# Gated delta rule on one core: squares of chunk outputs split in two parts and summed by two fp32r products

## The reference

```python
def step(state, xs):
    u_c, w_c, qd_c, kd_c, a_c, gl_c = xs
    v_new = u_c - w_c @ state
    o_c = qd_c @ state + a_c @ v_new
    state = state * gl_c + kd_c^T @ v_new
    return state, o_c
...
o = rmsnorm_2(o, out_norm) * silu(z)      # mean of squares over the 128 features of a head
return o.reshape(B, L, GDN_V_W) @ w_out
```

## Time and profile before

| | |
|---|---|
| median of 3 runs | 1943.84 us (1940.74 to 1944.12) |
| profiled execution | 1942.34 us, span 1939.6 us |
| TensorE busy | 1833.5 us, 95% |
| VectorE busy | 994.7 us, 51% |
| ScalarE busy | 822.8 us, 42% |
| GpSimd busy | 676.4 us, 35% |
| TensorE clock granted, mean | 0.985 |
| the four recurrences | 885 to 924, 1034 to 1086, 1197 to 1249, 1360 to 1412 us |

### The profile page before, as it was taken

One profiled execution on the slowest core, in us unless ns is written; L12 is line 12 of the kernel. 1 busy time (PEld: TensorE's weight loads), 2 busy tenths in 40 slices (PEclk: granted clock), 3 DMA queues, 4 the chain that ended last, 5 costly groups with the idle time before them and its releaser, 6 DMA issues.

```text
span 1939.6 us, 30688 instructions
## 1 busy us (share of the span) xinstructions
PE 1833.5 (95%) x11693; PEld 1538.4 (79%) x11829; DVE 994.7 (51%) x1753; ACT 822.8 (42%) x1503; POOL 676.4 (35%) x429
## 2 busy tenths in 40 slices
PE   6999999999999998998999999999978999999996
PEld 4777788888787876887989998998976667777776
DVE  6522233731111225665765774775766556566666
ACT  4566643352323233633633642562445443333433
POOL 3222244453534342270280263255224212222312
PEclk9999999999999998999999999999999999999998
DMA  5112133232323230420230131122132101221201
GB/s 186 55 55 66 55 98 109 66 98 68 118 80 105 86 99 21 137 79 1 80 89 23 55 91 48 52 80 78 34 111 76 55 33 55 65 55 53 76 32 44
DMA packets 73668, 138.90 MB, mean 72 GB/s; under 512 B 30640, under 2 KB 42416, under 8 KB 73296
## 3 DMA queue, kind: packets, MB, share of 16 engines
q1 hardware_dynamic: 72976, 132.41, 22.7%
q10 hardware_dynamic: 576, 4.87, 0.6%
HBM read 127.62 MB, written 9.63 MB: 71 GB/s over the span
## 4 chain that ended last, share of the span: by engine, by line
PE 44%; DVE 6%; POOL 5%; issue 3%; ACT 3%; DMA 0%; SPq 0%; ACTq 0%; POOLq 0%; DVEq 0%
PE ps L348 9%; PE ps L350 8%; PE ps L349 8%; PE ps L3092 4%; PE ps L3048 2%; POOL wsp L343 2%; PE ps L3055 2%; PE ps L3082 1%; POOL ov L836 1%; PE ps L2770 1%; POOL work L832 1%; PE ps L2874 1%; PE ps L2907 1%; PE ps L2912 1%; DVE aux_f L1789 1%
## 5 line engine op out<-in xcount | busy, mean ns | idle before, releaser
L343 POOL TENSOR_TENSOR wsp<-raw,wsp 128x1024 fp32r<-128x1024 f32 x228 | 549.8, 2418 | 1154.7 <-ACT wsp L338 1154.5
L348 PE MATMUL ps<-h_split,wsp 128*128 128x264 f32 (+2 forms) x1552 | 535.0, 345 | 16.8 <-DVE h_split L497 5.0
L349 PE MATMUL ps<-h_split,wsp 128*128 128x264 f32 (+2 forms) x1552 | 516.0, 332 | 0.0
L350 PE MATMUL ps<-h_split,wsp 128*128 128x264 f32 (+2 forms) x1552 | 515.6, 332 | 0.0
L348 PEld LDWEIGHTS ps<-h_split,wsp 128*128 128x128 f32 x1552 | 294.3, 190 | 58.2 <-issue 17.2
L349 PEld LDWEIGHTS ps<-h_split,wsp 128*128 128x128 f32 x1552 | 295.3, 190 | 28.8 <-issue 0.2
L350 PEld LDWEIGHTS ps<-h_split,wsp 128*128 128x128 f32 x1552 | 294.2, 190 | 29.2
L338 ACT ACTIVATE wsp<-raw 128x1024 fp32r<-128x1024 f32 x228 | 237.6, 1050 | 95.2 <-PE ps L350 94.5
L348 PE MATMUL ps<-y_split,wsp 128*128 128x512 f32 (+2 forms) x512 | 196.4, 384 | 11.5 <-DVE y_split L531 5.3
L349 PE MATMUL ps<-y_split,wsp 128*128 128x512 f32 (+2 forms) x512 | 192.5, 376 | 0.0
L350 PE MATMUL ps<-y_split,wsp 128*128 128x512 f32 (+2 forms) x512 | 192.0, 375 | 0.0
(11 more groups left out here) (391 smaller groups left out, 2929.6 us busy)
## 6 DMA issues: line engine op xcount, KB each, us to landing
raw<-in_w SPq DMA_DIRECT2D x228, 512.0 KB, 3.5
m_home<-ov SPq DMA_DIRECT2D x16, 256.0 KB, 3.5
x_home<-x_res ACTq DMA_DIRECT2D x1, 2112.0 KB, 6.9
x_res<-in_x SPq DMA_DIRECT2D x4, 512.0 KB, 5.3
out<-x_res SPq DMA_DIRECT2D x16, 128.0 KB, 1.7
x_res<-x_home ACTq DMA_DIRECT2D x1, 1584.0 KB, 7.4
mats<-in_mats SPq DMA_DIRECT2D x1, 640.0 KB, 7.4
x_res<-x_home ACTq DMA_DIRECT2D x1, 528.0 KB, 3.9
```

The lines of the kernel that those rows point to most:

```text
L343: pool.tensor_tensor(wsp[:, s, 1, :], raw[:, s, :], wsp[:, s, 0, :].bitcast(F32), ALU.subtract).then_inc(lo_ready, 1)
L348: pe.matmul(o, wh, xh, start=start, stop=False)
L349: pe.matmul(o, wh, xl, start=False, stop=False)
L350: return pe.matmul(o, wl, xh, start=False, stop=stop)
```

## The change

After the square, ScalarE copies it to an fp32r buffer `sq_hi`, VectorE subtracts that from the square into `sq_lo` (in place of the square), and TensorE sums both with a matrix of -1 in fp32r, in two products of all four heads at once instead of four fp32 products. The factor -1/128 goes into the logarithm's scale. `sq_hi` lies where RO lies, so the copy waits for the store of the chunk before. VectorE does its part for chunk c-1 behind VB of chunk c (and behind `copy_z(3)` for c = 1), ahead of R, and for the last chunk ahead of the four gate products. The semaphore of the last quarter of x is shared with that of x's copy to DRAM, whose waits count up to 32.

```diff
+        sq_hi, sq_lo = quad(yt, 6 * 512), quad(yt, 5 * 512)
...
+        def x_part(q):
+            return sem("x_moved") if q == 3 else sem(f"x_in{q}")
...
-                sp.dma_start(X[:, 2 * q:2 * q + 2, META:T], A["x"][:, 2 * q:2 * q + 2, :]).then_inc(sem(f"x_in{q}"), 16)
+                sp.dma_start(X[:, 2 * q:2 * q + 2, META:T], A["x"][:, 2 * q:2 * q + 2, :]).then_inc(x_part(q), 16)
...
-            norm_squares(act, "n1", lambda k: X[:, k, REAL], N1, ready=lambda k: (sem(f"x_in{k // 2}"), 16))
+            norm_squares(act, "n1", lambda k: X[:, k, REAL], N1, ready=lambda k: (x_part(k // 2), 16))
...
-                    act.activation(RO[:, :, 0:n], bank(2, n), ACT.Ln, bias=col("eps")).then_inc(sem("g_oln"), 1)
+                    act.activation(RO[:, :, 0:n], bank(2, n), ACT.Ln, bias=col("eps"), scale=-1.0 / P).then_inc(sem("g_oln"), 1)
...
                     act.activation(SQO[:, :, 0:n], bank(4, n), ACT.Square).then_inc(sem("g_sqo"), 1)
+                    act.wait_ge(sem("g_sqo"), 2 * at - 1)
+                    if c:
+                        act.wait_ge(sem("g_store"), at - 1)
+                    act.activation(sq_hi[:, :, 0:n], SQO[:, :, 0:n], ACT.Copy).then_inc(sem("g_sqo"), 1)
...
-                    act.wait_ge(sem("x_moved"), 16)
+                    act.wait_ge(sem("x_moved"), 32)
...
+                def square_low(c):
+                    n = tokens(c)[1]
+                    at = gst(g, CHUNKS, c + 1)
+                    dve.wait_ge(sem("g_sqo"), 2 * at)
+                    dve.tensor_tensor(sq_lo[:, :, 0:n], SQO[:, :, 0:n], sq_hi[:, :, 0:n].bitcast(F32), ALU.subtract)\
+                       .then_inc(sem("g_sq_lo"), 1)
...
                     if c:
+                        square_low(c - 1)
                         dve.wait_ge(sem("g_ks"), later)
...
+                square_low(LATER)
                 for t in range(4):
                     gate_y(t, LATER - 1)
                 add_out(6)
...
-                    pe.wait_ge(sem("g_sqo"), at)
+                    pe.wait_ge(sem("g_sqo"), 2 * at)
...
-                    for h in range(HG):
-                        last = pe.matmul(quads(2, h, P, n), mat(MEAN_128), SQO[:, h, 0:n], start=True, stop=True)
-                    last.then_inc(sem("g_on"), 1)
+                    total = PS[:, 2, :].rearrange("p (h n) -> p h n", h=HG)[:, :, 0:n]
+                    pe.matmul(total, ones_r[:, 1, :], sq_hi[:, :, 0:n], start=True, stop=False)
+                    pe.wait_ge(sem("g_sq_lo"), at)
+                    pe.matmul(total, ones_r[:, 1, :], sq_lo[:, :, 0:n], start=False, stop=True)\
+                      .then_inc(sem("g_on"), 1)
```

## The result

| | before | after |
|---|---|---|
| median | 1943.98 us (20 runs) | 1949.98 us (1940.98 to 1955.99, 20 runs) |
| ratio, 95% interval | | 1.0035 [1.0024, 1.0046] |
| profiled execution, span | 1942.34, 1939.6 us | 1949.95, 1947.9 us |
| granted clock, mean of that execution | 0.985 | 0.980 |

The change costs 6.0 us by the medians. The forecast was no change, 1943.7, within 1939.8 to 1948.0. The page of the changed kernel shows no sign of more work: TensorE's busy time is the same as before to 0.7 us, in 120 records less.

A forecast was written before the change was run, and what follows sets the result against it. TensorE was taken as the bound. Group 0's +0.9 us and -1.0 for groups 1 to 3 gave -0.1 against 1942.34, so 1942.2; with the median 1.5 above that execution, 1943.7, range 1939.8 to 1948.0.

The forecast's parts named there:

- 0.86: Norm pair on TensorE: upper bound in us if its two products stand alone between waits; 0.46 was forecast.
- 1.8 was summed: Groups 1 to 3, up to the last chunk: shorter norm products in line on TensorE save 1.8 us per group.
- rival (b): Norm pair not streamed, costs up to 0.86 us, so groups 1 to 3 save nothing on norms: 1949.2 us; chance 0.12.
- The gap of VectorE: Group 0, chunks 1 to 3: VectorE idles 0.73 us between VB and L2018; the new difference fits there, costing nothing.
- the 1.46 us that were drawn: Ends of groups 1 to 3: gates queue behind square, copy and difference, so add and TensorE come 1.46 us later.
- 0.16 and 0.75: Group 0: chunk 4 longer by 0.16 us, and TensorE freed 0.75 us later at the group's end.
- (a): Full gain: the gates' wait at the ends of groups 1 to 3 costs nothing; -4.5 us, 1939.3; chance 0.12.
- (c): Difference or gates meet GpSimd's L343 at three ends, up to 2.1 us each: 1945 to 1950 us; chance 0.06.
- rival (d): TensorE idles 2.4 us at three ends and its clock falls, 3.1 us each: 1953 us; chance 0.04.
- -1.8 + 1.46 = -0.34 per group: Groups 1 to 3: saving on the norms plus later end, net -0.34 us per group, -1.0 for three.
- -0.1: Whole kernel: group 0's +0.9 us and -1.0 for groups 1 to 3 sum to -0.1 us.

The follow-up runs named there:

- group 0 old: Changed kernel with group 0's four fp32 products and no split as in the kernel before, gates ahead of the add: 1950.70 us, ratio 1.0033.
- late gates: Kernel before, four fp32 norm products kept, but VectorE waits for the last square and does two 128x512 operations before the gates: 1950.22 us, ratio 1.0038.

## Why the prediction was wrong, point by point

- **The work: right.** The pair costs 0.47 us in line and not 0.86: the steps gained 1.83 where 1.8 was summed, so rival (b) falls. The gap of VectorE held the difference in group 0 (its second and third step take 9.13 us before and after). The end of a group is later by the 1.46 us that were drawn, group 0 by 0.24 and 0.81 instead of 0.16 and 0.75. (a) falls, since the gates stood behind the last square; (c) didn't come, no gate met GpSimd's subtraction: all of these gates took 0.63 us.
- **The step that failed** is the price of the pause, which rival (d) had named, and with it "-1.8 + 1.46 = -0.34 per group". The pause of TensorE was forecast at about 2.4 us (2.30 came), but its worth was taken as its length, and a fall of the clock behind it was put at nothing in the sum. Behind pauses of 2.29 to 2.64 us the clock fell in eleven of twelve cases (two profiles of the changed kernel, one with group 0 old, two of three ends with late gates), and each fall cost 1.3 to 1.6 us, about as much as the delay of 1.46 itself. So an end costs +2.75 to +3.01 and not +1.46, and a group is +0.9 to +1.2 and not -0.3. With the pauses filled the loss was gone (1.0000).
- **Why (d) got 0.04.** Group 0 was read as proof that pauses are harmless, since it kept clock 1.00 over gaps that were put at 1.5 us; the longest in that trace is 1.40. At the ends of groups 1 to 3 that holds for such lengths: no fall stood behind pauses of 0.43 to 1.58 us in fifteen cases. It said nothing of 2.3. And it was one execution: four later profiles with that same group 0 have a fall in it. The Trainium skill, TensorE: Matmul & The Clock Gate, Part 1, has half speed as the default that activity lifts; the falls behind 2.3 us side with it, and the row was used against it outside its range.
- **The price in (d) was too high,** 3.1 us from a mixed stretch, where 1.3 to 1.6 is what an output tile loses. With the right price and all three falls, the sum would have been -0.1 + 4.2, 1947.9; the measured median is 1950.0. The other 2 us stay open. In the profiles there are more stretches of half clock elsewhere: at 15 to 26 us, long before any new product, the clock reads 0.69 in the changed kernel and 1.00 before. Why isn't shown.

## What to carry to other kernels

A pause of the matrix engine costs its length and then, where the clock falls behind it, a stretch of half clock too: before you let one grow, look how long the others are and what clock follows them, and don't take a proof for short pauses as one for long. In an in-order queue put first what another engine waits for (the add) and what fills time last (the gates). A change that gains where an engine is in line belongs only there; where it is hidden (group 0) it brings only its new waits, here 1.05 us by the rows. And place a loss in the whole trace before you give it to the piece that you changed: falls of the clock move from one place to another between kernels.

## What the runs showed of the hardware

- TensorE's clock has two levels, 1.2 and 2.4 GHz, in the stretches of 1 us above (0.50 and 1.00, or a mix). At the ends of groups 1 to 3 it fell late in the pause or up to 1 us behind it. In the changed kernel's group 2 the stretch 1250 to 1251 us reads 0.90, and TensorE resumes at 1251.27. With late gates TensorE resumes at 1083.95 and products are 0.19 to 0.22 us apart from 1084.42; in group 3 it resumes at 1414.51, and the clock reads 1.00 up to 1415 and 0.77 in the next stretch. So it was the work behind the pause that paid.
- Adding eight useless products of 0.23 us to TensorE at each of three places brought the ratio to before from 1.0035 to 1.0000.
- A pause of 2.64 us once had no fall behind it, while pauses of 2.63 us in the same execution had.
- Single executions spread over 15 us in the changed kernel (1941 to 1956) and 12 in the kernel before (1937 to 1949), and go with the mean clock: correlation -0.96 and -0.85.
